# Layer 0's attention-gate sum from VectorE to GpSimd, and four pieces of VectorE's queue in another order

## What is computed

```
c_act = jax.nn.silu(c)
for l in range(DEPTH):
    mod = (c_act @ ada_w[l] + ada_b[l])[:, None, :]
    sh1, sc1, gt1, sh2, sc2, gt2 = jnp.split(mod, N_MOD, axis=-1)
    h = rms_norm(x, norm1_g[l]) * (1.0 + sc1) + sh1
    x = x + gt1 * token_mixer(h, ...)          # q_lat, kv_lat, k_rope, dq, dk, dv, conv, gates = split(h @ w_in)
    h = rms_norm(x, norm2_g[l]) * (1.0 + sc2) + sh2
    x = x + gt2 * conv_gated_mlp(h, ...)
return rms_norm(x, final_g)
# in token_mixer
q = rms_norm(q_lat, q_norm_g) @ w_uq;  kv = rms_norm(kv_lat, kv_norm_g) @ w_ukv
k_pe = apply_rope(k_rope[:, None], cos_r, sin_r)
qd, kd = apply_rope(dq), apply_rope(dk)        # differential attention
```

## Time and profile before

| | |
|---|---|
| median of 3 runs | 969.6 us (967.64 to 969.62) |
| the profiled execution, its own time | 969.08 us |
| its span, first to last instruction | 967.3 us |
| TensorE (matmuls) busy | 943.4 us, 98% |
| VectorE busy | 788.4 us, 82%, 1168 instructions |
| ScalarE busy | 517.8 us, 54% |
| GpSimd busy | 18.1 us, 2%, 23 instructions |
| mean granted TensorE clock | 0.994 of full speed |

### The profile page before, as it was taken

How to read it: one execution, slowest core, us unless ns; L and a number is a source line. 1 busy time by engine, 2 the same in 40 slices (tenths; PEclk the granted TensorE clock), 3 DMA queues, 4 the chain that set the end, 5 groups by cost and what they waited for, 6 DMA issues and landing times.

```text
span 967.3 us, 18684 instructions
## 1 busy us (share of the span) xinstructions
PE 943.4 (98%) x7695; PEld 904.2 (93%) x7695; DVE 788.4 (82%) x1168; ACT 517.8 (54%) x725; POOL 18.1 (2%) x23
## 2 busy tenths in 40 slices
PE   5899999999999999999999999999999999999997
PEld 3798899999998999999989999999999899999997
DVE  2589999978985888889895799999898688888643
ACT  3475456557345666654255655565844456665432
POOL 5000000000000000000000000000000000000001
PEclk9999999999999999999999999999999999999999
DMA  9996555666783565957994654456678455555551
GB/s 309 336 313 189 176 189 166 201 224 211 259 296 112 191 194 194 331 174 284 392 356 132 196 146 140 142 157 206 217 262 302 132 174 181 193 192 175 175 175 44
DMA packets 142515, 204.07 MB, mean 211 GB/s; under 512 B 3928, under 2 KB 114660, under 8 KB 142436
## 3 DMA queue, kind: packets, MB, share of 16 engines
q1 hardware_dynamic: 142100, 202.78, 62.6%
q10 hardware_dynamic: 336, 0.14, 0.1%
HBM read 199.76 MB, written 1.05 MB: 208 GB/s over the span
## 4 chain that ended last, share of the span: by engine, by line
PE 79%; DVE 15%; DMA 2%; ACT 2%; issue 1%; SPq 0%; DVEq 0%
PE PB L1619 17%; PE PB L1621 16%; PE PB L1620 16%; DVE wL L1039 5%; DVE buf L1145 3%; PE PB L1642 2%; PE PB L1643 2%; PE PB L1644 2%; PE SC L1621 2%; PE SC L1619 2%; PE SC L1620 2%; PE ST L1598 2%; DMA raw<-in_w_in 1%; DMA ada_pre<-in_ada_w 1%; PE TR L1621 1%
## 5 line engine op out<-in xcount | busy, mean ns | idle before, releaser
L1619 PE MATMUL PB<-hH,wH 128*128 128x256 f32 x1360 | 388.9, 286 | 0.7 <-DVE wL L1039 0.7
L1621 PE MATMUL PB<-hH,wL 128*128 128x256 f32 x1360 | 384.8, 283 | 0.0
L1620 PE MATMUL PB<-hL,wH 128*128 128x256 f32 x1360 | 384.7, 283 | 0.0
L1039 DVE TENSOR_TENSOR wL<-raw,wH 128x2048 fp32r<-128x2048 f32 (+3 forms) x152 | 322.9, 2127 | 63.8 <-ACT wH L742 59.5
L742 ACT ACTIVATE wH<-raw 128x2048 fp32r<-128x2048 f32 (+3 forms) x152 | 268.4, 1782 | 106.5 <-DMA raw<-in_w_down 53.1
L1619 PEld LDWEIGHTS PB<-hH,wH 128*128 128x128 f32 x1360 | 260.7, 192 | 3.1 <-issue 1.7
L1620 PEld LDWEIGHTS PB<-hL,wH 128*128 128x128 f32 x1360 | 260.8, 192 | 0.1
L1621 PEld LDWEIGHTS PB<-hH,wL 128*128 128x128 f32 x1360 | 260.7, 192 | 0.0
L1145 DVE SCALAR_TENSOR_TENSOR buf<-G,vec,buf 128x256 f32<-128x256 f32 x240 | 98.2, 480 | 0.3
L1399 DVE SCALAR_TENSOR_TENSOR ups<-PB,vec,ups 128x254 f32<-128x254 f32 (+1 forms) x176 | 72.6, 475 | 18.0 <-ACT ups L910 18.0
L918 ACT ACTIVATE gH<-ups 128x512 f32 (+1 forms) x22 | 13.9, 632 | 86.7 <-DVE ups L1406 86.7
(11 more groups left out here) (302 smaller groups left out, 1698.4 us busy)
## 6 DMA issues: line engine op xcount, KB each, us to landing
raw<-in_w_in SPq DMA_DIRECT2D x48, 1024.0 KB, 5.6
raw<-in_w_up SPq DMA_DIRECT2D x44, 1024.0 KB, 5.1
ada<-in_ada_w SPq DMA_DIRECT2D x35, 1024.0 KB, 8.5
raw<-in_w_down SPq DMA_DIRECT2D x22, 1024.0 KB, 4.9
ada_pre<-in_ada_w SPq DMA_DIRECT2D x8, 1024.0 KB, 13.5
raw<-in_w_o SPq DMA_DIRECT2D x8, 1024.0 KB, 6.3
raw<-in_w_out_diff SPq DMA_DIRECT2D x4, 1024.0 KB, 4.9
raw<-in_w_out_conv SPq DMA_DIRECT2D x4, 1024.0 KB, 5.0
```

The lines of the kernel that those rows point to most:

```text
L1039: dve.tensor_tensor(wL[s][:, 0:size], raw[s][:, 0:size], wH[s][:, 0:size].bitcast(F32), ALU.subtract).then_inc(w_lo[s], 1)
L1619: pe.matmul(out, a, xh(k), start=first and k == 0, stop=False, skip_group_check=True)
L1620: pe.matmul(out, a, xl(k), start=False, stop=False, skip_group_check=True)
L1621: ins = pe.matmul(out, b, xh(k), start=False, stop=last and k == kt - 1, skip_group_check=True)
```

## The change

GpSimd now makes the whole gate sum of layer 0, with fifteen instructions in place of VectorE's eight: per tile it multiplies either row by its column of `c_col`, adds the two, and from the second tile on adds the sum of the tile before. In VectorE's stream the rope of the latent key moves from step 7 to step 3, ahead of chunk 5's low half, the latent reciprocal to the head of step 4, the rope of the first differential keys from the end of step 5 to its head, and, in layer 0 alone, the row maxima of D0 ahead of the low half in step 6; in step 17 the weights of M0 stand ahead of the low half. Other than the gate sum and the maxima of D0 these moves are made in both layers.

```diff
-ROTATE_AT = {4: ["Rq0"], 5: ["Rk0"], 7: ["Rkr"], 9: ["Rq1"], 10: ["Rk1"], 15: ["RM0"], 20: ["RM1"], 25: ["RM2"],
+ROTATE_AT = {4: ["Rq0"], 9: ["Rq1"], 10: ["Rk1"], 15: ["RM0"], 20: ["RM1"], 25: ["RM2"],
...
+            pool.wait_ge(s_silu, 1)
+            for i in range(4):
+                w = early_ws[i]
+                pool.wait_ge(early_in[i], 16)
+                pool.tensor_scalar(w[:, 0, :], w[:, 0, :], c_col[:, 2 * i, 0:1], None, ALU.mult)
+                link(pool.tensor_scalar(w[:, 1, :], w[:, 1, :], c_col[:, 2 * i + 1, 0:1], None, ALU.mult))
+                ins = pool.tensor_tensor(w[:, 0, :], w[:, 0, :], w[:, 1, :], ALU.add)
+                if i:
+                    link(ins)
+                    ins = pool.tensor_tensor(w[:, 0, :], w[:, 0, :], early_ws[i - 1][:, 0, :], ALU.add)
+                ins.then_inc(early_added, 1)
+                pool.wait_ge(early_added, i + 1)
...
             def mixer_step(l, n):
                 if n == 3:
                     latent_squares(l)
-                if l == 0:
-                    early_steps(n)
-                if n == MLA + 1:
+                    if l == 0:
+                        lam_sums()
+                        flush_vectors(l)
+                        dve.wait_ge(s_table, 1)
+                    rope(l, "Rkr")
+                if n == 4:
+                    dve.wait_ge(st_read, FREE + l * len(ST_USES) + 2)
+                    link(dve.reciprocal(rdev[:, :], rdev[:, :]))
+                if n == 5:
+                    rope(l, "Rk0")
+                if n in (MLA + 1, MLA + 4):
                     weights(l, SCORES_AT[n - 1])
+                if l == 0 and n == 6:
+                    row_max(l, SCORES_AT[n])
                 if n < OUTS:
                     low(l, n + 2)
-                if l == 0 and n == 3:
-                    lam_sums()
-                    flush_vectors(l)
-                if l == 0 and n == 4:
-                    dve.wait_ge(s_table, 1)
                 if l == 0 and n == 5:
                     lam_end()
                 ada_work(l, n)
-                if n - 1 in SCORES_AT and n != MLA + 1:
+                if n - 1 in SCORES_AT and n not in (MLA + 1, MLA + 4):
                     weights(l, SCORES_AT[n - 1])
...
             def reduce_early():
 
-                after(early_added, 8)
+                after(early_added, 4)
```

More of the change, by code:

```diff
@@ L118 @@
 EARLY_Q = 0
-EARLY_LOADS, EARLY_STEPS = [3, 4, 4, 5], [2, 2, 3, 3, 3, 3, 4, 4]
+EARLY_LOADS = [3, 4, 4, 5]
 LATE_Q = 2
@@ L1216, in mixer_step @@
                     rope(l, use)
-                if n in SCORES_AT:
+                if n in SCORES_AT and (l, n) != (0, 6):
                     row_max(l, SCORES_AT[n])
                 if n == 5 - l:
-                    dve.wait_ge(st_read, FREE + l * len(ST_USES) + 2)
-                    link(dve.reciprocal(rdev[:, :], rdev[:, :]))
                     for k in range(QT + KVT):
@@ L1302, in mixer_step @@
                         merged_low(l, n)
[L1304 to L1317, removed]
             def late_steps(l, n):
```

## The result

The changed kernel takes **981.45 us** (median of 4 runs, 980.6 to 981.7), the kernel before in the same rounds 969.2 us: ratio 1.0127, 95% interval 1.0114 to 1.0139, slower by 12.2 us. The sign was right; the forecast of 995.0, +25.4 us, was twice too large. The profiled execution took 981.3 us (span 979.5), 12.2 us over the one of before.

A forecast was written before the change was run, and what follows sets the result against it. TensorE was bound by small stops behind VectorE's unpausing queue, 4.6 us in all. GpSimd's holds of VectorE stop it 28.5 us, less 4.6 gained, plus 1.5 of clock: +25.4 on 969.6, 995.0 us, range 964.0 to 1002.0.

The forecast's parts named there:

- What bounds the kernel; the gains: TensorE's stops behind VectorE's queue: 3.8 us in layer 0 and 0.8 in layer 1 go, 4.6 us gained.
- Durations on GpSimd: Gate sum at 128x1024: multiplication 2.8 us (ends 1.23 and 3.7), addition 2.33, about 40 us in all from 48.6.
- estimate of 1.05 us: The skill's price for one GpSimd multiplication at 1024 columns; by it the result would come out near 981.
- Taken to the new place: From 49 us, VectorE's short instructions each wait out a GpSimd one; chunk 5's low half ends at 95.3 us.
- term of 28.5 us of stops: TensorE's stop up to chunk 5, wanted at 66.79 us: 28.5 us in all, 6.5 of it at the latent squares.
- By then GpSimd is done: After chunk 5's low half GpSimd no longer holds VectorE; chunk 6 follows in time and 4.6 us are gained.
- Half clock: After TensorE's long stop, one stretch at the lower clock level: 12 matmuls of 0.12 us, 1.5 us.
- The sum: Whole kernel: 28.5 - 4.6 + 1.5 = +25.4 us, 995.0 us for the median.
- The milder hold: Rival: two short VectorE instructions pass between two of GpSimd's (985), or multiplications cost near 1.23 us (982); chance 0.20.
- The hold does not carry over: Rival: long GpSimd instructions let VectorE's through or hold them only briefly, so gains stand: 965.0 us; chance 0.18.

The follow-up runs named there:

- no_sum: The changed kernel without GpSimd's fifteen instructions, the gate sum of layer 0 left out on either engine: 964.54 us.
- order_only: The changed kernel with the gate sum back on VectorE in its old steps, all other moves kept: 968.53 us.
- two_op: The changed kernel with GpSimd's eight multiplications each written as two operations in one instruction (times the column, plus 0.0): 975.41 us.
- only_add: The changed kernel with GpSimd's seven additions alone, its eight multiplications left out: 974.25 us.
- only_mult: The changed kernel with GpSimd's eight one-operation multiplications alone, its seven additions left out: 964.64 us.
- sum_only: The changed kernel with VectorE's other instructions in the order of before, the gate sum still on GpSimd: 981.55 us.
- spread: The changed kernel with the sum on VectorE, five of its eight instructions in steps 9 to 11, eight layer 0 convolution taps in steps 17 to 20: 965.28 us.
- few_moves: The kernel before with M0's weights first, latent key's rope in step 12 (both layers), diff pair 0 keys' rope first in layer 1's step 5: 971.95 us.

## Why the prediction was right in sign and wrong in size

- **What bounds the kernel; the gains.** Right in the mechanism: the stops of the earlier trace rows are what there was to gain, and in no_sum all are gone. The size (4.6 us forecast, 4.7 measured) fits partly by luck, as said there. order_only shows that VectorE had no room ahead of chunk 5.
- **Durations on GpSimd.** Right: multiplication 2.8 forecast, 2.85 measured unheld; addition 2.33 and 2.40; start at 48.6 and 48.40. The estimate of 1.05 us after the Trainium skill (GPSIMD Engine Reference, section 3.1) fits only the two-operation form, 1.12 us here. With it the prediction would have said 981, close to 981.45, for the wrong reason: two_op, which has those multiplications, takes 975.4.
- **"Taken to the new place"**, the step that failed. It made each of GpSimd's fifteen instructions hold VectorE for its whole length, one for one, so that chunk 5's low half ended at 95.3. It ended at 73.5. The term of 28.5 us of stops came out as 10.1, 4.5 of it up to chunk 5. The seven additions do hold so (2.40 us, each with one VectorE instruction); the eight multiplications hold 1.1 of 2.9 us, and several short VectorE instructions pass in the rest. The earlier trace rows had additions alone on GpSimd, and the step carried them over to multiplications. The Trainium skill (SBUF — State Buffer, "SBUF: two separate sides") has the pair of ports locked for the whole instruction; the additions and the two-operation multiplications agree, the one-operation ones do not.
- **"By then GpSimd is done."** Wrong as a consequence: VectorE came to chunk 5's low half with eight additions and multiplications still to go, and they made the stops at the scores and at chunks 7 and 8 (2.19, 1.03, 2.38) that were forecast as none.
- **Half clock.** Forecast once, 1.5 us. The four longer stops drew three stretches, together about 5 us (the stops at 89.57 and 91.84 share one); nearly as much as the 5.5 us that the stops have grown by.
- **The sum.** The forecast was 13.2 us too high: 18.4 too much in the stops, less 3.5 to 4 too little in the clock, less 1.8 for a later start that it did not have. So the error of the failed step was larger than the error of the result, and part of the agreement that is left is luck.
- **The rivals.** The milder hold (985, stops of 10 at chunk 5 and 10 later) was nearer to what happened, in its time and in having stops behind chunk 5, though not by its reason. "The hold does not carry over" is true of the multiplications alone.

What stays open: why a one-operation multiplication of 2.9 us lets go after 1.1; and in part why identical code ahead of 44 us ends at another time from kernel to kernel (43.20 in only_add, 44.41 before, 46.90 in only_mult, rows of TensorE with the same 0.59 us wait). The granted clock of the first 44 us accounts for much of it: the change, sum_only, only_mult and spread had 0.84 and start at 46.2 to 46.9 us, the kernel before 0.92, only_add 0.96. But no_sum had 0.92 and starts at 46.00, and two_op had 1.00 and starts at 45.18, so it is not all, and what makes the clock differ there no run shows. Since only_mult starts late and is among the fastest, this is not what the sum costs.

## What to carry to other kernels

Work moved to GpSimd is not free for a VectorE that runs without a pause: count GpSimd's additions of two tiles and its two-operation multiplications, and charge each with its full length to the next VectorE instruction that it meets, of the kinds seen held here (instructions with two tiles as input, copies, multiplications by a column); cut the additions into slices if they must stay. Look first for a later stretch in which VectorE itself has room: here the same order with five sums and eight taps in later steps of VectorE's gains 4 us, with GpSimd it loses 12. And reckon behind every new stop of TensorE with a stretch at half clock, about 1.5 to 2.3 us where one came; one long stop (two_op) was cheaper here than four shorter ones of the same sum (the change).

## What the runs showed of the hardware

- **A one-operation multiplication by a column** on GpSimd (128x1024) takes 2.85 us and holds VectorE about 1.1 us; with a second operation in the same instruction it takes 1.12 us and holds for all of it. The second operation makes it 2.5 times faster; neither form costs the kernel anything measurable alone (964.64 and 964.55 us against 964.54 without).
- **Not every VectorE instruction is held.** The latent reciprocal takes 3.34 us at 77.50 in two_op, beside an addition of GpSimd's that ends at 79.80, and 3.35 in the kernel before, with GpSimd idle.
- **GpSimd is held as well.** A low half of VectorE's that came first makes a multiplication of 2.85 us last 4.76 to 5.02 us in the change.
- **Clock after a stop.** Stops as short as 1.03 and 2.19 us together were followed by a stretch in which the granted clock fell to 0.5: 91.80 to 97.00 us at 0.67 in the mean, 30 matmuls where 45 fit. The length of a stop alone does not decide it: 1.65 us in few_moves drew such a stretch, 1.72 us before the change and 3.52 us in only_add did not.
